# Two transformer blocks with mixtures of experts: the last four blocks' rows summed by a weighted one-hot product, the other rows read back among the last weights

## The reference

```python
def run_block(args):
    xe, e = args
    return (jax.nn.silu(xe @ w_gate[e]) * (xe @ w_up[e])) @ w_down[e]
...
y = jnp.zeros((n_tok + 1, d), yb.dtype).at[slot_tok].add(yb * slot_gate[:, None])
...
x = x + hierarchical_moe(h2, ...)
```

## Time and profile before

| | us |
|---|---|
| runs shown | 1792.24, 1801.91, 1895.73 |
| median | 1801.91 |
| the profiled execution | 1801.99 |
| its span | 1800.0 |

### The profile page before, as it was taken

How to read it: one execution, slowest core, us unless ns; L and a number is a source line. 1 busy time by engine, 2 the same in 40 slices (tenths; PEclk the granted TensorE clock), 3 DMA queues, 4 the chain that set the end, 5 groups by cost and what they waited for, 6 DMA issues and landing times.

```text
span 1800.0 us, 35945 instructions
## 1 busy us (share of the span) xinstructions
PE 1540.7 (86%) x15248; PEld 939.5 (52%) x15248; DVE 706.2 (39%) x1473; ACT 504.3 (28%) x1055; POOL 88.1 (5%) x86
## 2 busy tenths in 40 slices
PE   7999999698988999999599997999697978777771
PEld 3455554455555655666455547965454545444440
DVE  3378341432212111312468937642542433222324
ACT  3233671235423332332348411232010100000001
POOL 0000000000000000000000023100000000000000
PEclk9999999799999999999799998999698998888886
DMA  9274531579899999999570091045799999999994
GB/s 367 99 264 158 183 147 47 184 304 407 366 400 418 417 418 414 414 416 406 194 280 1 4 134 56 4 172 234 271 413 424 423 423 425 424 424 423 422 393 183
DMA packets 100210, 520.04 MB, mean 289 GB/s; under 512 B 19179, under 2 KB 25163, under 8 KB 67288
## 3 DMA queue, kind: packets, MB, share of 16 engines
q1 hardware_dynamic: 92280, 500.40, 70.5%
q0 software_dynamic: 7776, 17.37, 2.6%
HBM read 503.74 MB, written 24.95 MB: 294 GB/s over the span
## 4 chain that ended last, share of the span: by engine, by line
PE 48%; DMA 32%; issue 9%; DVE 6%; SPq 2%; ACT 2%; DVEq 0%; ACTq 0%; POOLq 0%
DMA ring<-in_w_up 18%; PE bank L900 13%; PE bank L484 8%; DMA arena<-in_w_up 6%; PE bank L492 5%; PE bank L916 5%; PE bank L848 3%; DMA ring<-in_w_down 2%; DMA arena<-in_w_down 2%; PE bank L715 2%; DMA arena<-xnd,smalli 1%; PE bank L550 1%; PE bank L477 1%; DVE arena L2676 1%; DMA ring<-diag 1%
## 5 line engine op out<-in xcount | busy, mean ns | idle before, releaser
L900 PE MATMUL bank<-ring,arena 128*32 128x256 f32 x5664 | 418.1, 415 | 94.9 <-DMA ring<-in_w_up 71.1
L900 PEld LDWEIGHTS bank<-ring,arena 128*32 128x32 f32 x5664 | 216.0, 119 | 229.2 <-issue 136.7
L2437 DVE TENSOR_TENSOR arena<-arena,bank 64x256 f32<-64x256 f32 x108 | 45.7, 423 | 542.2 <-ACT arena L1868 542.1
L484 PE MATMUL bank<-arena,ring 128*128 128x512 f32 x560 | 245.7, 595 | 0.0
L1868 ACT ACTIVATE arena<-bank 64x256 f32<-64x256 f32 x108 | 40.6, 376 | 509.4 <-PE bank L900 509.2
L484 PEld LDWEIGHTS bank<-arena,ring 128*128 128x128 f32 x560 | 105.8, 191 | 128.1 <-issue 128.1
L916 PE MATMUL bank<-ring,arena 128*32 128x256 f32 x2592 | 158.1, 384 | 2.5 <-DMA ring<-in_w_down 2.5
L900 PE MATMUL bank<-arena 128*32 128x256 f32 x1248 | 133.5, 434 | 29.8 <-DMA arena<-in_w_up 18.4
L492 PE MATMUL bank<-arena 128*128 128x128 f32 x880 | 112.7, 281 | 0.0
L492 PEld LDWEIGHTS bank<-arena 128*128 128x128 f32 x880 | 103.4, 192 | 15.3 <-issue 14.2
L2414 DVE TENSOR_TENSOR arena<-bank,arena 32x256 f32<-32x256 f32 x224 | 94.2, 420 | 42.9 <-PE bank L916 39.7
(11 more groups left out here) (436 smaller groups left out, 1773.7 us busy)
## 6 DMA issues: line engine op xcount, KB each, us to landing
ring<-in_w_gate SPq DMA_DIRECT2D x54, 2048.0 KB, 15.8
ring<-in_w_up SPq DMA_DIRECT2D x53, 2048.0 KB, 19.3
ring<-in_w_down SPq DMA_DIRECT2D x48, 2048.0 KB, 17.4
arena<-in_w_down SPq DMA_DIRECT2D x16, 2048.0 KB, 41.0
ring<-in_w_mod SPq DMA_DIRECT2D x12, 2048.0 KB, 15.3
arena<-in_w_up SPq DMA_DIRECT2D x11, 2048.0 KB, 34.3
ring<-in_w_in SPq DMA_DIRECT2D x10, 2048.0 KB, 17.3
arena<-in_w_gate SPq DMA_DIRECT2D x10, 2048.0 KB, 32.6
```

The source lines that it names most:

```text
L484: mm = pe.matmul(b[:, 0:n], w[:, k, col:col + P], ap[:, k, :], start=(k == 0), stop=(k == KD - 1))
L900: mm = pe.matmul(GU[CAP * i:CAP * i + CAP, 0:256], x, w[:, c, col:col + 256], start=(c == 0), stop=(c == KD - 1), skip_group_check=True)
L2437: TTo(hb, sg, GU[2 * CAP:4 * CAP, 0:256], ALU.mult).then_inc(S("h_done"), 1)
```

## The change

- The last quad's rows are not scattered. Its weights are spread into `hot`, for each tile of tokens a matrix of rows by tokens that holds a row's weight at its token (L2579, four DVE instructions), and PE multiplies it with `ys` (L1024, 8 products of 128x128 by 128x512). DVE adds the sums to x (`add_last`).
- The other rows are loaded by the same 8 loads, but in SP's order ahead of the last two down weights, and added on DVE in the last block (`add_early`, 8 instructions as before, L2588). A pair whose row lies in the last quad, or in an overflow block, has the weight 0 there; its row of yd holds a copy of the input x, which four copies of 2.1 MB from DRAM to DRAM put there early in the kernel, since it must be finite.
- The overflow's loop stands in an `If` that each engine asks once.
- In the second MoE x stays in its area. There are nine buffers for ten, and neither a save nor a reload of x.
- The table BESIDE puts all 64 context steps ahead of the last four experts.
- In the router the product that the first gather needs stands ahead of those for the ranks, and some ten small DVE instructions are added after it.

```diff
-NOV = 31
+NOV = 32
...
-_whole, _done, _blocks = BLOCK_US * NB[0] + STEP_US * CONTEXT_STEPS, 0, 0
+LATE, LASTQ = 4, sum(SIZES[0][-4:])
+_whole, _done, _blocks = BLOCK_US * (NB[0] - LASTQ) + STEP_US * CONTEXT_STEPS, 0, 0
...
-    _due = round((_whole * (_p + 1) / NE - BLOCK_US * _blocks) / STEP_US)
+    _due = round((_whole * min(1, (_p + 1) / (NE - LATE)) - BLOCK_US * min(_blocks, NB[0] - LASTQ)) / STEP_US)
...
-        NBUF = 10
-        SPOT = [0, 1, 2, 3, 4, 6, 7, 5, 9, 8]
-        ARENA = [0, 3, 2, 1]
+        NBUF = 9
+        SPOT = [0, 1, 2, 3, 4, 6, 7, 5, 8]
+        ARENA = [0, 3, 2]
...
-                with nc.tensor.Fori(0, (NOV + 1) // 2) as i:
-                    for q in range(2):
-                        with pe.If(n_over > i * 2 + q):
...
+                with nc.tensor.Fori(0, 1) as none:
+                    with pe.If(n_over > none):
+                        with nc.tensor.Fori(0, NOV // 2) as i:
+                            for q in range(2):
...
+                pe.wait_ge(S("placed"), 4 * m + 4)
+                pe.wait_ge(S("xs_ready"), 2 * (g0 + NQ[m]))
+                for t in range(TT):
+                    for half in range(2):
+                        b = V.deal(pe, f"last{m}{t}{half}")
+                        pe.matmul(b[:, :], hot[:, P * t:P * t + P], last_ys(m)[:, 512 * half:512 * half + 512],
+                                  start=True, stop=True).then_inc(V.full, 1)
...
+            for y in yd:
+                for k in range(2):
+                    sp.dma_start(y[T * k:T * k + T, :], a["x"]).then_inc(S("rows_in"), 16)
+
             sp.wait_ge(V.free, V.at("mod11"))
...
-            def save_x(t):
-                sp.wait_ge(V.free, V.at(f"outB1{t}"))
-                sp.dma_start(x2d[P * t:P * t + P, :], x_tok[:, t, :]).then_inc(S("x2_out"), 16)
...
+                    if (j, p) == (2, NE - 2):
+                        for u in range(2):
+                            sp.wait_ge(S(f"stored{u}"), 16 * stores(m + 1, u))
+                        if m:
+                            sp.wait_ge(*spent(1, 1, NE - 3))
+                        else:
+                            sp.wait_ge(CV.full, CV.at(f"SU{2 * TC - 1}"))
+                        load_y(m, yg if m else yg2)
                     load_e(m, i, expert.get(p))
 
-                if m:
-                    sp.wait_ge(*spent(1, *STREAM[1][XLAST]))
-                    sp.dma_start(x_tok, x2d.rearrange("(t p) d -> p t d", p=P)).then_inc(S("x_again"), 16)
...
-                scatter(NQ[m] - 2)
-                scatter(NQ[m] - 1)
-                pool.sem_inc(S("yd_done"), 1)
...
+                def spread():
+                    if m == 0:
+                        dve.wait_ge(CV.full, CV.at(f"SU{2 * TC - 1}"))
+                    for t in range(TT):
+                        ins = TS(hot[:, P * t:P * t + P], pcol("io128", 0, P), last_tok[:, t:t + 1], last_w, ALU.is_equal, ALU.mult)
+                    ins.then_inc(S("placed"), 1)
+
+                def add_early():
+                    tiles = yg if m else yg2
+                    for t in range(TT):
+                        dve.wait_ge(S(f"y_in{t}"), 16 + 32 * (m + 1))
+                        o = x_tok[:, t, :]
+                        for k in range(2):
+                            chain(STT(o, tiles[t][k], w12_early[:, TT * k + t:TT * k + t + 1], o, ALU.mult, ALU.add))
...
+                    if n == NB[m] - 3:
+                        spread()
+                    if n == NB[m] - 1:
+                        add_early()
...
+            def add_last(m, t):
+                done = S("x4_ready" if m else "x2_ready")
+                o = x_tok[:, t, 0:512]
+                TTo(o, take(f"last{m}{t}0")[:, :], o, ALU.add).then_inc(V.free, 1)
+                o = x_tok[:, t, 512:1024]
+                TTo(o, take(f"last{m}{t}1")[:, :], o, ALU.add).then_inc(done, 1)
+                dve.wait_ge(done, t + 1)
+                dve.sem_inc(V.free, 1)
```

More of the change, by code:

```diff
@@ L176, in build @@
         nega = small(8)
-        w12 = small(8)
-        assert max(NBLK) <= 46 and NOV + 1 <= 32
+        w12, w12_early, s12_kept, w12_late, w12_none = (small(8) for _ in range(5))
+        last_tok, last_w, edge = small(TT), small(1), small(1)
+        assert max(NBLK) <= 46 and NOV + 1 <= 33
         slots_any = smalli[:, 0:46]
@@ L351, in build @@
         PARTS = [(0, 0, D), (1, 0, D), (2, 0, D), (3, 0, D // 2), (3, D // 2, D)]
-        yg = [[area(2 - 2 * (t // 2), 2048 * (t % 2) + 1024 * k, 1024) for k in range(2)] for t in range(TT)]
-        m5, b5, fgrow = area(5, 2144, 256), area(5, 3840, 256), area(3, D, D)
+        assert [SPOT[STREAM[1].index((j, NE - 3)) % NBUF] for j in range(2)] == [RING + 1, RING - 1]
+        yg = [[(ring[:, (RING - 1) * UNIT + o:(RING - 1) * UNIT + o + 1024] if t // 2 else area(3, o, 1024))
+               for k in range(2) for o in [2048 * (t % 2) + 1024 * k]] for t in range(TT)]
+        yg_late = [[area(3 * (t // 2), 2048 * (t % 2) + 1024 * k, 1024) for k in range(2)] for t in range(TT)]
+        hot = area(5, 2560, T)
+        m5, b5, fgrow = area(5, 2144, 256), area(5, 3840, 256), area(2, 0, D)
         hT0 = chunks(area(0, 0, 4096), T)
@@ L370, in build @@
         diag_r = chunks(area(4, 0, TT * P), P)
-        yg2 = [[ring[:, o:o + 1024] for k in range(2) for o in [(5 - 5 * (t // 2)) * UNIT + 2048 * (t % 2) + 1024 * k]]
-               for t in range(TT)]
+        yg2 = [[area(2 - 2 * (t // 2), 2048 * (t % 2) + 1024 * k, 1024) for k in range(2)] for t in range(TT)]
         junk = area(5, 1536, D)
@@ L446, in stores, with last_ys @@
         def stores(m, q):
-            return sum(len(range(q % 2, NQ[i], 2)) for i in range(m)) + q // 2
+            return sum(len(range(q % 2, NQ[i] - 1, 2)) for i in range(m)) + q // 2
+        def last_ys(m):
+            return ys[(NQ[m] - 1) % 2]
         def beside_now(n, at):
@@ L1021, in moe @@
                 mm.then_inc(V.full, 1)
+                pe.wait_ge(C.free, len(C.names))
+                b = CV.deal(pe, f"soon{m}")
+                pe.wait_ge(S("placed"), 4 * m + 1)
+                for t in range(TT):
+                    for e in range(2):
+                        mm = pe.matmul(b[2 * CAP * e:2 * CAP * e + 2 * CAP, 0:1], in_soon[:, TT * e + t, :], pcol("tokg", t),
+                                       start=(t == 0), stop=(t == TT - 1), skip_group_check=True)
+                mm.then_inc(CV.full, 1)
                 b = V.deal(pe, f"order{m}")
@@ L1027, in moe @@
                   .then_inc(V.full, 1)
-                pe.wait_ge(C.free, len(C.names))
-                b = CV.deal(pe, f"soon{m}")
-                pe.wait_ge(S("placed"), 3 * m + 1)
-                for t in range(TT):
-                    for e in range(2):
-                        mm = pe.matmul(b[2 * CAP * e:2 * CAP * e + 2 * CAP, 0:1], in_soon[:, TT * e + t, :], pcol("tokg", t),
-                                       start=(t == 0), stop=(t == TT - 1), skip_group_check=True)
-                mm.then_inc(CV.full, 1)
                 b = V.deal(pe, f"homes{m}")
@@ L1478, in _ @@
             experts(1)
-            sp.wait_ge(C.free, len(C.names))
-            sp.wait_ge(S("y_taken"), BASE[1] + NB[1])
-            for u in range(2):
-                sp.wait_ge(S(f"stored{u}"), 16 * stores(2, u))
-            sp.wait_ge(S("yd_done"), 2)
-            load_y(1, yg)
+            sp.wait_ge(*spent(1, 2, NE - 1))
             sp.dma_start(fgrow, a["fg"].partition_broadcast(P)).then_inc(S("rows"), 16)
@@ L2497, in experts @@
                 own(f"rank{m}")
+                TS(slots_any[:, 0:1], take(f"soon{m}", CV)[:, 0:1], NOWHERE, T - 1.0, ALU.add, ALU.min).then_inc(CV.free, 1)
                 b = take(f"order{m}")
@@ L2505, in experts @@
                 dve.sem_inc(V.free, 1)
-                TS(slots_any[:, 0:1], take(f"soon{m}", CV)[:, 0:1], NOWHERE, T - 1.0, ALU.add, ALU.min).then_inc(CV.free, 1)
                 b = take(f"homes{m}")
```

317 lines of the change are left out of this document (168 added, 149 removed).

## The result

The changed kernel takes 1814.91 us at the median of 13 runs (1805.97 to 1826.07), the kernel before 1804.12 us in the runs beside it. The ratio is 1.0065, 95% interval [1.0042, 1.0087]: 0.65% or 11.7 us slower, where I had forecast 7.5 us faster. That lies inside 2%, but outside the range of 1778 to 1812.

The account below looks back on a forecast made before the run. The chain of waits gave PE 48%, DMA 32%, issue 9%; PE's backlog set the first MoE's end, the last weight the second's. From 1801.99 us, -7.0 - 0.8 + 0.3 = -7.5 gave 1794.5 us, range 1778 to 1812.

Parts of the forecast that it names:

- the steps that left the last blocks: First MoE: some nine context steps, 18 us of PE, done earlier within PE's waits for up weights (33.9 us); cost nothing.
- Rival 3: Added work is dearer: products at lower clock, moved steps uncovered (+8), or a dearer overflow jump; 1799.1 to 1812; chance 0.24.
- The asking: End of each MoE: the overflow is asked once, taken as 1.0 us, below two PE askings of 0.65.
- a jump of more than 2 us: Sign of a wrong prediction: the jump over the overflow's body costs more than 2 us.
- the tail: Ends of the MoEs: turning x 7.0 us earlier in the first; last weight to span's end 14.5 us shorter in the second.
- the lost slot: Second MoE's start: nine buffers for ten move each later load by a slot, +4.9 us on the last weight.
- the cost of the y rows in the queue: Both MoEs: 4.19 MB ahead of the last two downs take 10.05 us in the first, 9.9 in the second.
- the eight products: End of each MoE: eight added products of 128x128 by 128x512 on PE take 9.2 us.
- the copies: Early in the kernel: four copies of x to yd, 8.4 MB, take 20 us of an otherwise idle queue; no cost.
- the second MoE's last weight: Second MoE: it lands at 1761.0 + 4.9 + 9.9 - 1.2 = 1774.6.
- the row of 8.19 us: A profiled set of 16 product records, read as running soon after a pause; 7.03 us on a running PE.
- The net of the second MoE: Second MoE: later last weight against the shorter end (-14.5), given as -0.8 us.

## Why the prediction was wrong

**The step that failed** is in the first MoE: the steps that left the last blocks, "I cost this at nothing, the cover being those waits; without it up to 8 us would come back". The cover was taken over the wrong stretch, and the work was counted short. PE has 52 blocks of some 6.2 us, by the table's own figure, and 64 steps of 2.05, 453 us, beside 96 loads of 5.03 us, 483 us: 30 us of slack over the stage by this estimate, and the waits of 33.9 us are this slack. The new table wants the same 64 steps beside 28 experts. The old table puts 52 of them there, so twelve were moved, 24.6 us, and not nine. In that stretch the 47 blocks and 52 steps are 398 us and the 84 loads 423, which leaves 25; with all 64 steps it is 423 to 423. Nothing is left. What didn't fit into the waits (they gave up 9.6 us) kept buffers in use longer, and the queue has holes. Products that start after a wait run longer too (5.35 us in the row of 872.55, 3.66 where PE goes on); how much of the loss that makes is not shown. I priced 18 us of moved work against the whole stage's waits; I should have compared the work with the loads up to block 46. Measured by itself: +0.61%, 11 us. In the changed kernel more of it counts: the queue's end moves by 21 us, and the ten that PE's backlog hides in the table's own experiment are the ten in which the sum had put the y rows ("the last weight lands at about 872"; it lands at about 890). Rival 3 held the mechanism, with 8 us and behind a chance of 0.24.

**The asking** was sized 1.0 us. It was 7.7 in the first MoE and 1.7 in the second, and leaving it out on PE gave 6.3 us back, give or take 5. That a jump of more than 2 us would be a sign of being wrong, the prediction had said itself. The Trainium skill (Runtime: NRT & Kernel Launch, Instruction fetch mechanics) says that a taken branch to a target outside the fetched window waits for a fetch. I held the 31 short askings against it. In the first MoE the piece fetched in the gap of 9.30 us agrees with the page; in the second, with 3.50, no fetch is seen. The mean of 31 askings, all over the same code, couldn't tell what the first one costs.

**The asking's worth** was not separated. I gave the tail -7.0 and -14.5 us for all its parts together. Asking once alone is worth 12 to 13 us in the kernel before, without a y row or a product moved. With that, the table (+11), the nine buffers (+5) and the y rows ahead of the downs (+9.5, from the kernel with the rows behind), the parts make 11 - 12.4 + 5 + 9.5 = 13.1 us, and the whole measured 11.7; what is left for the one-hot product, about -1, is not measurable. This sum of parts that were measured in different surroundings is an account, not a proof; the 9.5 above all was measured with the new table, and the y rows ahead of the downs with the old table were not run.

**Right** were the lost slot (+4.9 forecast for the last weight, +5.0 measured in the whole), the cost of the y rows in the queue (10.8 and 10.5 us between the traces with and without them, for 10.05 and 9.9), the eight products (9.16 and 9.52 for 9.2), the copies (no cost), and the second MoE's last weight (13.2 us for 13.6). They stand in a sum whose two wrong terms lie ahead of them. In the size of the eight products there is some luck: the row of 8.19 us that it leaned on does not stand after a pause. PE is busy without a gap ahead of it, with 2.6 us of small products just before, and the granted clock was 0.62 at 938 to 941. The net of the second MoE in the sum adds up to -0.9, not -0.8; nothing hangs on that.

## What to carry to other kernels

Work that is moved into waits must be held against the slack of the stretch it is moved to: compare the engine's work with the transfers up to that point, since an average of waits over the stage may be the very slack that the old place left. Before a new way of doing a tail is built, take the cheapest part of it alone (here one question for thirty-one) and time it. A transfer that is needed last can stand behind the last weight where the chain behind that weight is as long as the transfer; here the y rows were worth 9.5 us there.

## What the runs showed of the hardware

From the evacuation's end to the next product PE took 0.40 us without a question, 1.7 to 2.0 us with a question and a taken jump over its branch where no instructions were fetched in the gap, and 7.7 and 7.8 where a piece of 16 KB came in. Copies from DRAM to DRAM ran near 400 GB/s (387 at 170 to 180), where the weights' loads had 417. Single executions of the same kernel lay up to 20 us apart (1805.97 to 1826.07).
